# Orders in a three-layer fp32 kernel: the LayerNorm's variance, the RWKV pairs, the attention heads and the entry of S5

## The chip, the cores and the metric

The kernel runs on one NeuronCore of a Trainium2 chip, as one launch. The metric is the device time of one execution in microseconds (us), the median over runs. The engines are TensorE (PE in the profile, with its weight loads as PEld), VectorE (DVE), ScalarE (ACT), GpSimd (POOL) and SyncE (SP), which here only issues DMAs.

## The reference, cut to what matters

Input is x with 512 tokens of 1024 channels. All is fp32.

```python
x = first_block(x, ...)     # gMLP branch and RWKV-7 branch side by side
# second_block, two layers, each x = layernorm(alpha * x + gate * mixer(h)):
# i = 0: MLA attention over 512 latent and 256 context tokens, 16 heads; gives x and ctx
# i = 1: S5, 128 groups of 16 channels, 64 complex states, both directions; gives x only

def _layernorm(x, g, b):
    mu = mean(x); var = mean(square(x - mu))
    return (x - mu) * rsqrt(var + eps) * g + b

# RWKV-7, per head, per token:  S = S*w + (S a) b^T + v k^T ;  y = S r
# MLA, per head:  q_abs = q_nope @ w_uk ; p = softmax([q_abs, rope(q_r)] . keys) ; o = p . ckv
# S5, per group and direction:
#   u, g = split(h @ w_in); x_t = lam_bar * x_{t-1} + b_bar u_t ; y = Re(c x) + d u
#   out = (glu(gelu(y)) * silu(g)) @ w_out
```

## The kernel before, in words

Activations lie channel-major: 128 channels on the partitions, tokens along the free axis, eight blocks (k = 0 to 7) for 1024 channels. Weights come as a stream of 512 KB pieces through a ring of six slots, loaded by SP in one fixed order (L3175); a load waits until the slot's former piece has been used. Each engine's program is written out by hand in its own order, and `at(...)` gives the semaphore value at which a named step is done. No planner sets the order: moving a line moves the work.

**LayerNorm** (three of them, `LayerNorm`). Sums over channels are matmuls with a matrix of ones (`ones_product`, L335). `centre_dve` (L371) subtracts the mean per block, ScalarE squares it (L380), GpSimd adds squares in pairs (`pairs_pool`, L347) and TensorE sums the results into the variance (`var_pe`); ScalarE takes the root (L385), VectorE the reciprocal (L391) and scales each block (L395). The second one works on 768 columns (512 latent, 256 context tokens), the others on 512.

**RWKV.** Pairs of heads i = 0 to 3 in a software pipeline: `rwkv_pe`, `rwkv_act` and `rwkv_dve` work in iteration i on the chunk products of pair i, the eight-step state chain of pair i - 1 (`state_pe` L1220, `state_dve_` L1227), the preparation of pair i + 1, and batches of vector rows (`vec_rows_pe` L292: row vectors of the modulation, turned into columns by `vec_turn_pe` L303 and added by `vec_add_dve`). An iteration begins with four products (`products_pe`, L1026); VectorE masks them (`z0_dve`, RBT at L1163), and `akt_pe` (again L1026) waits for that. It ends with `gn_spread_pe` (L854), `gn_scale_dve` (L1300) and `gn_gain_act` (L1306), which finish the group norm of the pair before, and with the third vector batch. `rwkv_last_*` follow after iteration 3.

**Heads.** 16 heads, six units each: two units of 128 context queries and four of latent queries. Per unit TensorE makes scores (L2158, L2169), VectorE the maximum (L2275), ScalarE the exponential (L2295), VectorE the normalisation; TensorE turns the probabilities (`turn`, L2182) into PSUM banks 6 and 7, ScalarE copies them (`pt_act`: L2305 for the two context units, L2310), and TensorE multiplies by the values (L2193). The projection of the next head but one is woven in: fold (L2225), q_abs (L2229, copied by ScalarE at L2322, 768 columns) and rope (L2236). Both context units are turned into bank 6, so the second waits for the copy of the first. VectorE and GpSimd make S5's tables in the heads' free time; the products of b and powers of lambda are made per tile by `b_pow_dve` (L2019), stored to HBM by `b_pow_pool` (L2006) and loaded back for each tile of S5 by SP (L3081, 1 MB a tile).

**End of MLA.** The output projection (L2411), mean, then on VectorE: lags of tile 0 (`lags_dve`, L2650, L2653), one half of `b_pow_dve` for tile 15 (six 128x512 operations), centring, the other half, reciprocal. GpSimd's pair sums come before its last store; its memset (L2013) after all stores are done releases S5.

**S5.** 16 tiles m of 128 channels, each with four pairs n = 4m + pair. At the entry the scaled blocks are split into a rounded part and a rest (`s5_start_act`, L2497, L2501; `s5_start_dve`, L2523, L2515), and TensorE projects tiles 0 and 1 as they come (`u_project_pe`, L2575; 48 matmuls a tile, three products of hi and rest). Weights are rounded by ScalarE (L436) and their rests made by GpSimd (L448), two units a tile (`u_round_act`). ScalarE copies a projected tile to SBUF (`u_act`, L2590, L2592), SP stores it (L2604) and loads it transposed (L2613, eight DMAs). Per pair: `turn_pe` (L2669) transposes b powers, `x_pe` (L2715) makes the inputs of the states, `state_dve` (L2732 to L2752: multiply, scan, multiply) runs the recurrence, `y_pe` (L2769 with c powers; L2774 with u and the lag matrix) makes the output. The tile's lag matrix goes over HBM: TensorE (L2637), VectorE's copy (L2650), SP's store (L3154), and after it eight loads (L3161) that the tile's first L2774 waits for. In tile m TensorE also projects tile m + 2, split over the pairs by `TOKENS`; in tiles 14 and 15 these are the first two gate tiles (`gate_ahead_pe`). After the tiles come gates, GLU and output projection (L459), with ln3 at the end.

SP's program per tile: the 1 MB load of b powers for tile + 1, the lag store, the lag loads, u's store, c powers, table, u's loads, the ring's next piece.

## Time and profile before

| what | value |
|---|---|
| median of 3 runs | 2307.03 us (2306.19 to 2311.86) |
| profiled execution: own time, span | 2303.04 us, 2301.3 us |
| mean granted TensorE clock | 0.979 |
| busy: TensorE, VectorE, ScalarE, GpSimd | 93%, 58%, 34%, 27% of the span |
| first, second, third LayerNorm in the trace (us from the start) | 461 to 477, 1322 to 1355, 2276 to 2295 |
| RWKV iterations | 215 to 405 |
| heads | 692 to 1156, a head every 28.02 |
| S5 tiles | 1397 to 1742, a tile every 21.7 (first four), then 22.1 to 22.9 |
| after them: gates, GLU, output | 1749 to 2276 |

A row of a timeline reads: start, duration, engine, line, operation, what it writes <- what it reads, shape, how many; in brackets the idle time of the engine before it and what released it. A row of waits is: engine, waiting line <- releaser and its line, us in total, times, longest. PEclk is the share of the full TensorE clock (2.4 GHz) that was granted; 0.50 is the lower level. Durations of pipelined matmuls have modelled ends.

### The profile page before, as it was taken

What the parts mean: (1) busy time and instruction counts of PE and PEld (TensorE: products, weight loads), DVE (VectorE), ACT (ScalarE), POOL (GpSimd) and SP (SyncE); (2) the same over time, 40 slices, a digit from 0 to 9 for tenths busy, and PEclk for the clock granted to TensorE, in tenths of its full rate; (3) what the DMA queues carried; (4) which work ended last, traced back from release to release, by engine and by line L of the source; (5) the groups of instructions that cost most, each with busy time, mean ns of one, the idle gap of its engine ahead of it and who ended that gap; (6) DMA issues with size and microseconds to landing.
All of it is one profiled execution on the core that took longest, in us unless ns stands there. A gap on an engine that the chain in (4) does not pass through costs nothing.

```text
span 2301.3 us, 39928 instructions
## 1 busy us (share of the span) xinstructions
PE 2146.7 (93%) x15738; PEld 1559.2 (68%) x15738; DVE 1323.9 (58%) x2344; ACT 785.7 (34%) x1433; POOL 621.8 (27%) x1126
## 2 busy tenths in 40 slices
PE   6998998999998999999899958999998999999996
PEld 6876877755554555555455537888876788888784
DVE  2266664469994444444389877888884333333244
ACT  1335543231103444444300065454443423222223
POOL 0553211500017888888302111111110000000001
PEclk9999999999999999999999978999999999999998
DMA  8321443423451111111055316888874233333220
GB/s 309 101 90 57 150 150 119 159 82 115 170 188 56 67 53 51 51 54 67 35 207 182 144 61 188 257 248 264 247 235 176 83 93 100 94 98 100 93 92 37
DMA packets 105721, 294.58 MB, mean 128 GB/s; under 512 B 12608, under 2 KB 49728, under 8 KB 97088
## 3 DMA queue, kind: packets, MB, share of 16 engines
q1 hardware_dynamic: 93184, 227.02, 30.6%
q0 software_dynamic: 12352, 65.02, 7.5%
q8 instruction: 125, 2.05, 0.4%
q14 instruction: 60, 0.49, 0.1%
HBM read 225.01 MB, written 66.98 MB: 127 GB/s over the span
## 4 chain that ended last, share of the span: by engine, by line
PE 72%; DVE 13%; DMA 7%; issue 3%; ACT 3%; SPq 2%; POOL 0%; ACTq 0%; DVEq 0%; POOLq 0%
PE psum L459 29%; PE psum L2411 7%; PE psum L2193 4%; PE psum L2158 4%; DMA lags<-const 4%; DVE area L1933 3%; PE psum L2575 3%; PE psum L1040 3%; PE psum L2169 3%; PE psum L2236 2%; DVE dve_tmp L1933 2%; PE psum L2229 2%; PE psum L292 2%; SPq L3161 2%; PE psum L2182 2%
## 5 line engine op out<-in xcount | busy, mean ns | idle before, releaser
L459 PE MATMUL psum<-split,w_split 128*128 128x512 f32 x1632 | 373.2, 390 | 3.7 <-DVE w_split L441 3.7
L459 PEld LDWEIGHTS psum<-split,w_split 128*128 128x128 f32 x1632 | 307.4, 188 | 68.2 <-DVE w_split L441 4.1
L441 DVE TENSOR_TENSOR w_split<-ring,w_split 128x512 fp32r<-128x512 f32 x188 | 133.1, 708 | 319.0 <-ACT w_split L436 318.7
L1978 POOL TENSOR_TENSOR early<-early 128x8 f32<-128x8 f32 (+6 forms) x672 | 276.2, 411 | 52.8
L436 ACT ACTIVATE w_split<-ring 128x512 fp32r<-128x512 f32 x188 | 118.8, 632 | 349.4 <-PE psum L459 346.1
L1759 PE MATMUL psum<-early,ring 128*128 128x512 f32 (+1 forms) x544 | 176.5, 486 | 0.0
L2411 PE MATMUL psum<-gate,ring 128*128 128x512 f32 (+1 forms) x512 | 165.4, 486 | 1.2 <-issue 1.2
L2575 PE MATMUL psum<-h,u_w 128*128 128x256 f32 (+1 forms) x768 | 148.7, 347 | 14.1 <-ACT u_t L2497 13.6
L459 PE MATMUL psum<-h,w_split 128*128 128x512 f32 x624 | 148.2, 398 | 8.5 <-DVE w_split L441 8.5
L1759 PEld LDWEIGHTS psum<-early,ring 128*128 128x128 f32 x544 | 103.6, 191 | 71.8 <-issue 64.6
L2411 PEld LDWEIGHTS psum<-gate,ring 128*128 128x128 f32 x512 | 97.2, 190 | 69.3 <-issue 62.7
L459 PEld LDWEIGHTS psum<-h,w_split 128*128 128x128 f32 x624 | 118.4, 190 | 36.9 <-ACT w_split L436 5.4
L2575 PEld LDWEIGHTS psum<-h,u_w 128*128 128x128 f32 x768 | 119.7, 192 | 31.4 <-issue 14.9
L459 PE MATMUL psum<-h_split,in_w 128*128 128x512 f32 x600 | 139.1, 391 | 1.5 <-POOL in_w L448 1.5
L448 POOL TENSOR_TENSOR u_w<-ring,u_w 128x512 fp32r<-128x512 f32 x36 | 49.3, 1369 | 306.7 <-ACT u_w L436 306.4
L459 PEld LDWEIGHTS psum<-h_split,in_w 128*128 128x128 f32 x600 | 111.8, 188 | 27.2 <-ACT prev L704 2.1
L341 POOL TENSOR_TENSOR early<-xT 128x512 f32<-128x512 f32 x1 | 1.3, 1287 | 461.8 <-DVE xT L3052 461.8
L2275 DVE TENSOR_REDUCE early<-psum 128x1 f32<-128x768 f32 (+1 forms) x96 | 74.8, 780 | 75.6 <-PE psum L2169 73.6
L2158 PE MATMUL psum<-ckv,q_abs 128*128 128x256 f32 (+1 forms) x320 | 107.3, 475 | 5.9 <-ACT prob L2295 5.9
L448 POOL TENSOR_TENSOR in_w<-ring,in_w 128x512 fp32r<-128x512 f32 x50 | 77.2, 1543 | 125.8 <-ACT in_w L436 123.7
L2193 PE MATMUL psum<-area,ckv_tm 128*128 128x512 f32 (+1 forms) x256 | 102.8, 556 | 1.0 <-ACT area L2310 1.0
L2785 ACT ACTIVATE early<-psum 64x128 f32<-64x128 f32 x128 | 34.6, 270 | 159.7 <-PE psum L2774 100.5
(419 smaller groups left out, 3674.9 us busy)
## 6 DMA issues: line engine op xcount, KB each, us to landing
ring<-in_s_glu SPq DMA_DIRECT2D x64, 512.0 KB, 3.5
ring<-in_w_mod SPq DMA_DIRECT2D x48, 512.0 KB, 5.2
made_c_pow<-area POOLq DMA_DIRECT2D x16, 1152.0 KB, 5.2
c_pow<-made_c_pow SPq DMA_DIRECT2D x16, 1152.0 KB, 6.2
made_b_pow<-area POOLq DMA_DIRECT2D x16, 1024.0 KB, 4.6
b_pow<-made_b_pow SPq DMA_DIRECT2D x16, 1024.0 KB, 10.2
ring<-in_s_in SPq DMA_DIRECT2D x32, 512.0 KB, 6.1
ring<-in_w_in SPq DMA_DIRECT2D x29, 512.0 KB, 3.5
```

The lines of the kernel that those rows point to most:

```text
L436: nc.scalar.activation(rounded(buffer(u, 0)), source(u), ACT.Copy).then_inc(act_done, 1)
L441: nc.vector.tensor_tensor(rounded(buffer(u, 1)), source(u), buffer(u, 0), ALU.subtract).then_inc(dve_done, 1)
L448: nc.gpsimd.tensor_tensor(rounded(buffer(u, 1)), source(u), buffer(u, 0), ALU.subtract).then_inc(pool_done, 1)
L459: ins = nc.tensor.matmul(out, rounded(buffer(u, w)[:, ks]), values(x, k), start=(first and k == 0 and n == 0), stop=(last and k == UNIT_K ...
L1759: ins = nc.tensor.matmul(o, tile_w(("mla_in", m), k), h2[:, k, a:a + n], start=(k == 0), stop=(k == KD - 1))
L1933: nc.vector.tensor_tensor(o, a, b, op).then_inc(dve_done, 1)
L1978: nc.gpsimd.tensor_tensor(o, a, b, op).then_inc(pool_done, 1)
L2158: mm(o, q_abs_of(h, u), ckv[:, a:a + m], start=True, stop=False)
L2193: ins = mm(o, ckv_tm[:, k, :], pt[:, k, :], start=(k == 0), stop=(k == kt - 1))
L2275: v.tensor_reduce(sm[:, n % 3, 0:1], both(b)[:, 0:keys], AX.X, ALU.max).then_inc(dve_done, 1)
L2411: ins = nc.tensor.matmul(o, tile_w(("mla_out", 2 * m + k // KD), k % KD), gate2[:, k, a:a + n], start=(k == 0), stop=(k == KE - 1))
L2575: ins = nc.tensor.matmul(o, rounded(u_w[:, u % 4, w, kk * P:(kk + 1) * P]), h3_part(x, k)[:, a:a + size], start=(k == 0 and n == 0), stop= ...
```

## The change

Only orders, buffers and counts of small steps change; what is computed stays.

- **LayerNorm (all three).** GpSimd adds one pair of squares (4 and 5) instead of three pairs. TensorE sums seven blocks, in the order 0, 1, 2, 3, 6, the pair, 7, instead of five.
- **RWKV.** The turn of the third vector batch, its addition, and the spread, scale and gain of the group norm move from the end of an iteration behind the products (TensorE), behind z0 (VectorE) and behind the first `u_act_` (ScalarE) of the next one, or to the head of `rwkv_last_*`. State steps 1 to 3 are later in the order.
- **Heads.** The second context unit is turned into bank 7 and doesn't wait for the first one's copy. The copy of q_abs is two instructions (context 256 columns, latent 512); the first part of rope waits for the first only, the second part for both.
- **b powers of tile 15.** They are not made at MLA's end. `power_last_dve` keeps the powers in SBUF, SP loads b (b_last), and `b_pow_last_dve` makes the tile in SBUF in four groups of three 128x512 operations, behind the states of pairs 54 to 57 (tiles 13 and 14). The 1 MB store and load of that tile are gone. GpSimd adds ln2's squares after its last store has been issued.
- **S5 three tiles ahead.** TensorE projects tile 2 at the entry, before the first `x_pe`, and tile m + 3 in tile m; the gates come in tiles 13 and 14. ScalarE rounds unit 4 while the blocks are split, unit 5 between the copies of tiles 0 and 1, units 6 and 7 and the copy of tile 2 before `turn_act(1)`. GpSimd's rests and its y stores shift with that.

```diff
-    def pairs_pool(self, pool):
-        for j in range(KD // 2 - 1):
-            pool.wait_ge(*at(self.name, "sq", 2 * j + 1))
-            nc.gpsimd.tensor_tensor(self.sq[:, 2 * j, :], self.sq[:, 2 * j, :], self.sq[:, 2 * j + 1, :],
-                                    ALU.add).then_inc(pool_done, 1)
-            pool_count.up(self.name, "sq_pair", j)
+    def pair_pool(self, pool):
+        pool.wait_ge(*at(self.name, "sq", 5))
+        nc.gpsimd.tensor_tensor(self.sq[:, 4, :], self.sq[:, 4, :], self.sq[:, 5, :], ALU.add).then_inc(pool_done, 1)
+        pool_count.up(self.name, "sq_pair")
...
-        for j in range(KD // 2 - 1):
-            pe.wait_ge(*at(self.name, "sq_pair", j))
-            self.ones_product(self.var_bank, self.sq[:, 2 * j, :], j == 0, False)
-        for k in (KD - 2, KD - 1):
-            pe.wait_ge(*at(self.name, "sq", k))
-            ins = self.ones_product(self.var_bank, self.sq[:, k, :], False, k == KD - 1)
+        for k in (0, 1, 2, 3, 6, 4, 7):
+            if k == 4:
+                pe.wait_ge(*at(self.name, "sq_pair"))
+            else:
+                pe.wait_ge(*at(self.name, "sq", k))
+            ins = self.ones_product(self.var_bank, self.sq[:, k, :], k == 0, k == KD - 1)
...
     products_pe(pe, i)
+    if i > 0:
+        vec_turn_pe(pe, n0 - 1)
+    if prep:
+        prep_raw_pe(pe, i + 1)
+    if i > 1:
+        gn_spread_pe(pe, i - 2)
+    akt_pe(pe, i)
     if scan:
         state_pe(pe, i - 1, 1)
-    if prep:
-        prep_raw_pe(pe, i + 1)
-    akt_pe(pe, i)
+    vec_rows_pe(pe, n0, EARLY, *([("vec", n0 - 1, "added")] if n0 > FIRST_GATE else []))
+    u_pe(pe, i, 1)
     if scan:
         state_pe(pe, i - 1, 2)
-    vec_rows_pe(pe, n0, EARLY, *([("vec", n0 - 1, "added")] if n0 > FIRST_GATE else []))
-    u_pe(pe, i, 1)
     if prep:
         prep_k_ss_pe(pe, i + 1)
+    dz_pe(pe, i, 1)
     if scan:
         state_pe(pe, i - 1, 3)
-    dz_pe(pe, i, 1)
     vec_rows_pe(pe, n0, LATE)
...
         prep_turn_pe(pe, i + 1, 3)
-    if scan:
-        gn_spread_pe(pe, i - 1)
     if len(batches) == 3:
         vec_rows_pe(pe, batches[2], range(KD), ("vec", n1, "added"), *([("gn", i - 1, "std")] if scan else []))
-        vec_turn_pe(pe, batches[2])
...
-    if scan:
-        gn_gain_act(act, i - 1)
...
+    if i > 0:
+        vec_add_dve(dve, batches[0] - 1)
+    if i > 1:
+        gn_scale_dve(dve, i - 2)
+    zt0_dve(dve, i)
...
-    zt0_dve(dve, i)
+    if prep:
+        prep_scan_dve(dve, i + 1)
...
-    if prep:
-        prep_scan_dve(dve, i + 1)
...
+    vec_turn_pe(pe, TAIL_BATCH - 1)
+    gn_spread_pe(pe, q - 1)
...
-    for m in range(KE):
-        if m == KE - 1:
-            ln2.add_pool(pool, KD - 2)
-            ln2.pairs_pool(pool)
+    for m in range(KE - 1):
...
-        if m + 2 < KE:
+        if m + 2 < KE - 1:
...
-        if m % 2 == 1 and 5 <= m < KE - 1:
+        if m % 2 == 1 and 5 <= m:
...
+    ln2.add_pool(pool, KD - 2)
+    ln2.pair_pool(pool)
...
-        pool.wait_ge(b_pow_stored[i], 16 * KE // 2)
+        pool.wait_ge(b_pow_stored[i], 16 * (KE // 2 - i))
...
+power_last = const[:, len(MASKS) * P + N_LAGS + 8 * C_LAT + GS:][:, 0:2 * TPD * (STEP + 1)].rearrange(
+    "p (r t s) -> p r t s", r=2, t=TPD)
+b_last = const[:, len(MASKS) * P + N_LAGS + 8 * C_LAT + GS + 2 * TPD * (STEP + 1):][:, 0:N_B].rearrange(
+    "p (r t i) -> p r t i", r=2, i=GS)
...
+def power_last_dve(dve):
+    nc.vector.tensor_copy(power_last, power[:, :, tile_cols(KE - 1), :]).then_inc(dve_done, 1)
+    dve.wait_ge(dve_done, dve_count.up("s5", "power_last"))
...
+def b_pow_last_dve(dve, d, ri):
...
+    def tt(o, a, b, op):
+        nc.vector.tensor_tensor(o, a, b, op).then_inc(dve_done, 1)
+        dve.wait_ge(dve_done, dve_count.up("s5", "b_pow_last"))
...
+    if d == 0 and ri == 0:
+        dve.wait_ge(last_loaded, 16)
+        dve.wait_ge(*at("s5", "b_pow_t", TILE_PAIRS * (KE - 2) - 1))
+    shape = [P, TILE_PAIRS, STEP, GS]
+    part = s5_tmp[:, 0:TILE_PAIRS * STEP * GS].rearrange("p (t s i) -> p t s i", t=TILE_PAIRS, s=STEP)
+    idx = slice(7, None, -1) if d == 0 else slice(8, 0, -1)
+    pr, pi = (power_last[:, i, d::2, idx].unsqueeze(3).broadcast_to(shape) for i in range(2))
+    br, bi = (b_last[:, i, d::2, :].unsqueeze(2).broadcast_to(shape) for i in range(2))
+    out = b_pow[:, (KE - 1) % 2, ri, d::2, :, :]
+    if ri == 0:
+        tt(out, br, pr, ALU.mult)
+        tt(part, bi, pi, ALU.mult)
+        tt(out, out, part, ALU.subtract)
+    else:
+        tt(out, br, pi, ALU.mult)
+        tt(part, bi, pr, ALU.mult)
+        tt(out, out, part, ALU.add)
...
-        if n >= 1:
+        if n >= 1 and u != 1:
...
-            ins = nc.tensor.transpose(bank(6 + k // 3, (k % 3) * P, (k % 3 + 1) * P),
+            b = 6 + (u if u < 2 else k // 3)
+            ins = nc.tensor.transpose(bank(b, (k % 3) * P, (k % 3 + 1) * P),
...
-            pe.wait_ge(*at("q_abs", hh))
+            pe.wait_ge(*at("q_abs_ctx", hh))
...
+                if part == 1:
+                    pe.wait_ge(*at("q_abs", hh))
...
-                             bank(6, 0, 2 * P).rearrange("p (k c) -> p k c", k=2), ACT.Copy).then_inc(act_done, 1)
+                             bank(6 + u, 0, 2 * P).rearrange("p (k c) -> p k c", k=2), ACT.Copy).then_inc(act_done, 1)
...
-        nc.scalar.activation(q_abs[:, h % 2, :], both(0), ACT.Copy).then_inc(act_done, 1)
-        act.wait_ge(act_done, act_count.up("q_abs", h))
+        for (o, a, n), what in zip(parts_of(0), ("q_abs_ctx", "q_abs")):
+            nc.scalar.activation(q_abs[:, h % 2, a:a + n], o, ACT.Copy).then_inc(act_done, 1)
+            act.wait_ge(act_done, act_count.up(what, h))
...
             act.wait_ge(*at("s5", "h3", k - 2))
+        if k == 6:
+            u_w_act(act, 4)
         act.wait_ge(*at("ln2", "scaled", k))
...
         return
-    pe.wait_ge(*ready(b_pow_ready, m))
+    if m < KE - 1:
+        pe.wait_ge(*ready(b_pow_ready, m))
+    else:
+        pe.wait_ge(*at("s5", "b_pow_last"))
     if n == 0:
...
     turn_pe(pe, 0)
+    for k in range(KD):
+        u_project_pe(pe, 2, k)
     x_pe(pe, 0)
...
             for k in TOKENS[pair]:
-                u_project_pe(pe, m + 2, k)
+                u_project_pe(pe, m + 3, k)
             y_pe(pe, n)
...
     u_act(act, 0)
+    u_round_act(act, 5)
     u_act(act, 1)
...
         ln2_out_act(act, k)
-    u_round_act(act, 4)
-    u_round_act(act, 5)
+    u_round_act(act, 6)
+    u_round_act(act, 7)
+    u_act(act, 2)
     turn_act(act, 1)
...
-                u_round_act(act, 2 * (m + 3) + pair)
+                u_round_act(act, 2 * (m + 4) + pair)
...
-                u_act(act, m + 2)
+                u_act(act, m + 3)
...
-        if u % 2 == 1 and u >= 9:
-            y_store_pool(pool, u // 2 - 4)
-    for m in range(KE + GATES_AHEAD - 4, KE):
+        if u % 2 == 1 and u >= 11:
+            y_store_pool(pool, u // 2 - 5)
+    for m in range(KE + GATES_AHEAD - 5, KE):
...
+FIRST_LAST = TILE_PAIRS * (KE - 2) - 2
...
+            n = m * TILE_PAIRS + pair - FIRST_LAST
+            if 0 <= n < 4:
+                b_pow_last_dve(dve, n // 2, n % 2)
...
+            sp.dma_start(b_last, io["b_bar"][KE - 1].rearrange("p (r t i) -> p r t i", r=2, i=GS)).then_inc(last_loaded, 16)
...
-                b_pow_sync(sp, tile + 1)
+                if tile + 1 < KE - 1:
+                    b_pow_sync(sp, tile + 1)
...
+    power_last_dve(dve)
...
-    b_pow_dve(dve, KE - 1, (0,))
...
-    b_pow_dve(dve, KE - 1, (1,))
...
```

## Rows read from the trace of the kernel before

**Rows 1.** Span of the core and its granted TensorE clock.

```profile
...
core 0: 2301.3 us, clock 0.979
...
```

**Rows 2.** Page, parts 1 and 4: busy time by engine, then chain shares.

```profile
...
PE 2146.7 (93%) x15738; PEld 1559.2 (68%) x15738; DVE 1323.9 (58%) x2344; ACT 785.7 (34%) x1433; POOL 621.8 (27%) x1126
...
PE 72%; DVE 13%; DMA 7%; issue 3%; ACT 3%; SPq 2%; POOL 0%; ACTq 0%; DVEq 0%; POOLq 0%
...
```

**Rows 3.** PE's waits, whole run: line, releaser, us in total, times, longest.

```profile
...
PE psum L2575 <- ACT u_t L2497: 13.6, 1, 13.6
...
PE psum L2182 <- ACT area L2305: 10.3, 16, 2.4
PE psum L2774 <- DMA early<-lags: 9.9, 11, 2.3
PE psum L1026 <- DVE RBT L1163: 8.7, 4, 3.0
PE psum L335 <- POOL gate L347: 8.4, 1, 8.4
PE psum L2715 <- DMA u_t<-u_channels: 7.0, 1, 7.0
PE psum L2158 <- ACT prob L2295: 5.9, 16, 2.2
PE psum L2236 <- ACT q_abs L2322: 5.5, 16, 1.0
PE psum L335 <- POOL early L347: 4.0, 2, 3.7
...
```

**Rows 4.** Windows, S5 tiles 0, 7, 14: us, busy by engine, PEclk, DMA share, GB/s.

```profile
...
1396.92:1418.64 21.72, 21.72 (x250) 18.18 (x248) 17.58 (x41) 12.43 (x28) 2.62 (x2) 1.00 0.58 188
1550.64:1572.92 22.28, 21.79 (x248) 18.18 (x248) 18.86 (x47) 11.10 (x27) 3.30 (x3) 1.00 0.82 255
...
1708.27:1729.75 21.48, 19.15 (x224) 15.13 (x224) 18.37 (x51) 9.64 (x24) 2.45 (x3) 1.00 0.77 219
...
```

**Rows 5.** Timeline, start of an RWKV iteration: start, us, engine, line, idle before.

```profile
...
315.19 0.99 PE L1026 MATMUL psum<-a_cm,k_cm 64*64 64x64 f32 x32 [1.99 <-DVE RBT L1163]
...
```

**Rows 6.** Window over the RWKV iteration that begins there.

```profile
...
307.00:354.00 47.00, 42.81 (x1225) 37.33 (x1220) 30.08 (x56) 22.15 (x41) 9.01 (x10) 0.96 0.39 138
...
```

**Rows 7.** Timeline, first LayerNorm's variance.

```profile
...
467.79 4.46 PE L335 MATMUL psum<-sq,const 128*128 128x512 f32 x10
...
```

**Rows 8.** Timeline, third LayerNorm's variance.

```profile
...
2281.81 5.22 PE L335 MATMUL psum<-early,const 128*128 128x512 f32 x8 [0.26 <-POOL early L347]
...
```

**Rows 9.** Timeline inside one head.

```profile
...
903.87 0.44 PE L2182 MATMUL psum<-const,area 128*128 128x128 f32 x2 [0.52 <-ACT area L2305]
...
913.15 0.81 ACT L2322 ACTIVATE q_abs<-psum 128x768 f32<-128x768 f32 x1 [0.75 <-PE psum L2229]
...
```

**Rows 10.** Timeline, second LayerNorm up to the reciprocal.

```profile
...
1324.08 0.69 DVE L2019 TENSOR_TENSOR area<-area,power 128x512 f32<-128x512 f32 x1
...
1328.43 7.90 DVE L371 SCALAR_TENSOR_TENSOR early<-psum,early 128x768 f32<-128x768 f32 x8
...
1333.33 9.71 PE L335 MATMUL psum<-gate,const 128*128 128x256 f32 x20 [8.38 <-POOL gate L347]
...
1346.32 4.95 DVE L391 RECIPROCAL early<-early 128x768 f32<-128x768 f32 x1 [4.97 <-POOL area L2013]
...
```

**Rows 11.** Timeline in tile 7: a projection group, one operation's form alone and beside GpSimd.

```profile
...
1552.29 3.42 PE L2575 MATMUL psum<-h,u_w 128*128 128x256 f32 x18
...
1560.61 0.35 DVE L2724 TENSOR_TENSOR early<-early 128x192 f32<-128x192 f32 x1
...
1569.75 1.45 DVE L2724 TENSOR_TENSOR early<-early 128x192 f32<-128x192 f32 x1
...
```

**Rows 12.** SP's queue in the last tiles: lag store and lag loads.

```profile
...
1715.74 0.34 SPq L3154 DMA_DIRECT2D lags<-const  x1
1722.30 5.26 SPq L3161 DMA_DIRECT2D early<-lags  x8
...
```

More of the change, by code:

```diff
@@ L1431, in rwkv_act @@
             u_act_(act, i, 1)
+            if i > 1:
+                gn_gain_act(act, i - 2)
             if prep:
@@ L1564, in rwkv_last_act @@
             q = NPAIR - 1
+            gn_gain_act(act, q - 1)
             for k in range(3, 6):
@@ L1582, in rwkv_last_dve @@
             q = NPAIR - 1
+            vec_add_dve(dve, TAIL_BATCH - 1)
+            gn_scale_dve(dve, q - 1)
             for c in range(1, NCHUNK - 1):
@@ L2561, in u_project_pe @@
         def u_project_pe(pe, m, k):
+            if m >= KE + GATES_AHEAD:
+                return
             if m >= KE:
@@ L3061, in ln3_pool @@
                 ln3.add_pool(pool, k)
-            ln3.pairs_pool(pool)
+            ln3.pair_pool(pool)
         def ln3_pe(pe):
```

8 lines of the change are left out of this document (3 added, 5 removed).

## The prediction

> **What bounds the kernel now.** I read the span and granted clock first, then the page's busy shares and chain of waits, then TensorE's waits over the whole run, and only then timelines and windows around each edit. TensorE is busy 93% of the span, the clock is near full (0.979), and 72% of the chain that ended last is TensorE's [rows 1, 2]. So an edit is worth what it takes out of TensorE's idle time or puts into its work. The waits list shows how little idle there is and where it lies: one 13.6 us wait at the start of S5, one of 8.4 us in the second LayerNorm, one of 7.0 us for the transposed u, and many small ones in the heads, RWKV and the S5 tiles [rows 3]. The change touches nearly all of them. S5's tiles are not all alike: tile 0 has TensorE busy for its whole 21.72 us, tile 7 for 21.79 of 22.28 with the DMA engines 0.82 busy; there the late part is the load of the lag matrices, 9.9 us in 11 waits [rows 3, 4].
>
> **RWKV.** An iteration ends with the spread and scale of the pair before and with the turn of a vector row (`vec_turn_pe`), which waits shortly for ScalarE; in the next one `akt_pe` waits for VectorE's RBT: 1.99 us in the one shown, 8.7 us in four, the longest 3.0 [rows 3, 5]. The change puts the turn, the raw preparation and the spread behind the products, so their TensorE work fills the RBT wait. The spread is sixteen matmuls of the size of the 32 that took 0.99 us [rows 5], but narrow weights and twice the columns, so 1 us; the turn and its wait I take at 0.4 each: about 1.8 us an iteration where the wait is long enough. VectorE now runs z0 first and `gn_scale` (128x512, 0.69 us by the operation of that size in [rows 10]) after it, so RBT isn't later; but the scale delays the masks behind it (zt0) and the states. I take 0.75 for the iteration shown, 1.75 for each of the two after it, and some 1.6 for the clock: it stood at 0.96 over the 47 us shown [rows 6], which is 1.9 us a time, and it fell in just these idle gaps; I count one such loss and most of it again in the next; the last iteration loses 0.8, because the turn and spread now stand in front of its chain of state steps. Sum -5.0. Bounds: -6.5 (all four waits of 8.7 gone, less 2.2 for delayed masks) and -1.0 (the states, moved back on both engines, become what is late, so only the 0.40 waits go).
>
> **First LayerNorm.** Variance needs seven products instead of five. Ten matmuls took 4.46 us [rows 7], so one product (two matmuls) is 0.85 to 0.89. TensorE was the late engine there and stays it afterwards: +1.7; bounds 0 (if the last square was what held it) and +1.8. **Third LayerNorm.** Here the pair sum on GpSimd was late: two waits, 4.0 us together [rows 3], and the last eight matmuls took 5.22 us [rows 8], more than 8 x 0.446 = 3.6, a slow clock. Without the first two pair sums TensorE starts on single squares some 2 us sooner and ends, after 7 x 0.87 = 6.1 us, about 1.8 sooner. Bounds -2.3 and +0.8 (the same 7 products at the slower rate).
>
> **Heads.** Sixteen waits of `L2182` for the copy of the transposed probabilities (10.3 us, longest 2.4) come from two turns sharing one bank; the second turn gets its own bank and needn't wait. It is 0.52 us in the head shown [rows 9], of which I count 0.49: 15 x 0.49 + 0.65 for head 0, whose first turn is late for other reasons = 8.0. `L2236` waits for the whole copy of q_abs (5.5 us in 16) [rows 3]: the copy of 768 columns takes 0.81 us [rows 9]; its first third with a start cost will be ready some 0.4 sooner and the rope product needs only that: 15 x 0.28 + 0.43 = 4.6. Against it, ScalarE runs one more copy, about 0.17 to 0.2 us a head; it stands before the next exponential. TensorE reaches what follows later than ScalarE by about 0.5 us, which hides it. What is late next is `L2158` after the exponential, 5.9 us in 16, which I leave as it is. Sum -12.6; bounds -14 and -8 (every head gives back the extra copy and some 0.1 more at the exponential).
>
> **MLA's end.** The last b powers aren't made there: six VectorE operations of 0.69 us before the centring, and six after it, go, with their store [rows 10]. Added is one small copy at the start of the output projection, beside TensorE's own long work. Centring, which started at 1328.43, starts 3.4 us sooner, about 1325.05. The squares follow it at about 0.96 us each; seven products over 768 columns cost 7 x 0.89 x 1.5 = 9.3 us and start with the first square at about 1327: variance ends near 1336.6. Before, it began at 1333.33 behind the pair sums and ended at 1343.04, its twenty matmuls in 9.71 us where 5 x 1.33 = 6.7 would do, and the reciprocal then still waited for the store's memset until 1346.32 [rows 10]. Root and reciprocal now follow at about 1337.9: -8.4. If the clock falls in the sum, as it did before, half of that is lost, -4.3.
>
> **S5's entry.** The first projection starts 8.4 us sooner. TensorE then waited 7.0 us for u [rows 3]; now the whole projection of tile 2 stands in that wait. It is 48 matmuls, eighteen of which took 3.42 us with the modelled end of the last [rows 11], so 8.5 us: 1.5 beyond the wait. ScalarE gets a rounding step in its h chain (0.62 to 0.65, in one of the eight steps), and rounds and copies between the u copies. Against that, the x products and the first state group run without the slow clock that follows the idle 7 us, -2.1. The first y product, 1396.92 before (tile 0's window starts with it [rows 4]), comes at about 1387.9: -9.0 with the previous part. Bounds -10.5 and -4. Is it given back? The project work moved ahead leaves no shorter tile: in every tile TensorE does the same 48 matmuls for one tile further on, up to tile 12, and then the gates come one tile sooner. What remains unused is at tile 15, where VectorE holds the end anyway, so the gain stays until there.
>
> A collision counts here as well: the fifth rest on GpSimd (`L448`) now runs beside VectorE's h chain. In tile 7 a 128x192 operation of VectorE took 1.45 us with GpSimd's rest beside it, and 0.35 without [rows 11]. I leave it out of the sum and in the bounds: 1.1 once, with the start shared, 0.9.
>
> The Trainium skill, SBUF — State Buffer, "Who interferes with whom", says that a VectorE instruction with two SBUF inputs and a GpSimd instruction that reads SBUF exclude each other, and the later one waits for the whole of the first. The trace agrees with the 1.45 against 0.35. By this rule the moved rests would hit any such operation of VectorE, in the entry and in the tiles, which speaks against the change; by the rows the number of rests stays two a tile.
>
> **S5's end.** Twelve operations of 128x512, 0.69 us each [rows 10] plus gaps, 0.725: 2.18 a group, four groups in pairs 2 and 3 of tile 13 and 0 and 1 of tile 14. VectorE is busy 18.37 us in tile 14 and needs 4.4 more: 22.7 against its 21.48, with the state recurrence waiting behind each group [rows 4]. So this tile becomes VectorE-bound, +1.2 there, and +0.3 in tile 13. What is queued behind is the state group, TensorE's y product for it, and the copy of the last lags. The store of the last lags at 1715.74 is followed by loads only at 1722.30, 6.6 us later [rows 12], as the store's packets stood behind a 1 MB load of b powers, which is gone: that gives 2 to 5 us back to the last lag wait. I take -0.2 in all; bounds -2 and +5 (8.7 us less the 3 us that VectorE is idle in each tile, and no relief in the queue).
>
> **Sum.** -5.0 +1.7 -12.6 -9.0 -0.2 -1.8 = -26.9. The profiled execution took 2303.04 us, 1.74 around its span of 2301.3; it comes to 2276.1. The median of the runs shown is 2307.03, 4.0 above it, so 2280 is my number for the median.
>
> **Rivals.**
> (1) The lag chain keeps S5: in tiles 4 to 14 the DMA queue, not TensorE, sets the period [rows 4], and what the entry gains is partly taken by lags that land no sooner, and the b powers on VectorE cost the end 3.7 to 5. Then -26.9 + 4 to 5: -22, 2285. For it: the 9.9 us and DMA 0.82. Against it: the chain hangs on tile events that all move by the same 9 us.
> (2) The clock drops in the LayerNorm or the entry: -4.3 instead of -9.0, and in RWKV no relief (+1.6): -26.9 + 4.7 + 1.6 = -20.6, 2286. For it, the 9.71 us row [rows 10]; against it, TensorE is idle there for about 2 us only, not 8.
> (3) Heads keep their period, since the exponential's wait (`L2158`) takes up what the others give: -4 instead of -12.6: 2289. For it: ScalarE has one more instruction in front of the exponential. Against it: that wait is 5.9 us in 16 with one of 2.2 [rows 3], so about 0.25 in the others.
> (4) Slower than before: VectorE's chain becomes the bound of every S5 tile. It is busy 18.86 of 22.28 us [rows 4]; GpSimd's two rests a tile now start elsewhere, and each collision costs 1.1 [rows 11]. To cancel 27 us each of 16 tiles has to grow by 1.7, to 24.0, so that VectorE must lose 5.1 a tile, five collisions. With six a tile, 25.5 against 22.3 over the tiles, the time is 2303 - 27 + 51 = 2327 on the profiled execution; just past the point, 2310. For it: VectorE's slack is the smallest of the engines but TensorE's. Against it: there are two rests a tile, and one of them collides already.
>
> **How the numbers follow.** My forecast 0.55; rival 1 0.14, rival 2 0.12, rival 3 0.12, rival 4 0.04; and 0.03 for small gains that end up at no change. The range of the likeliest alone is 2274 to 2286. The range for the time is 2272 to 2291: it holds rivals 1 to 3 as well as several terms at their better end. A measurement of this kernel tells 0.3%, 7 us, from no change: faster 0.93, within 0.03, slower 0.04.
>
> **What would show it.** After: `L2182` no longer waits for `L2305` within a head, and the period of a head falls by about 0.77 (from 28.02); the `L1026` waits for RBT fall from 8.7 to under 4; the reciprocal `L391` of the second LayerNorm starts near 1338 less what RWKV and heads gave; no 7 us wait of `L2715`; first y product 25 us sooner than 1396.92; VectorE over 21 us busy in tile 14, and the lag store followed by its loads in under 4 us. Wrong if the head's period stays above 27.7, if the variance sum shows a clock of 0.5, or if tiles 1 to 12 are longer than 22.5 us.

## The result and the profile after

The changed kernel took 2283.27 us (median of 4 runs, 2279.60 to 2284.78), the kernel before 2308.28 in the runs beside it; the ratio is 0.9887, 95% interval 0.9863 to 0.9910, so 21 to 32 us less. Timed once more, it was 0.9891 (0.9873 to 0.9909). The forecast was 2280 in a range of 2272 to 2291. The profiled execution took 2281.87 us with a span of 2279.9. The total is right, in part by luck: several of its terms are off in opposite directions and cancel.

The first view is TensorE's waits over the whole run of the changed kernel: line <- what it waited for, us in total, times, longest. Line numbers have moved: L2620 was L2575, L2817 was L2769, L2195 was L2158, L1025 was L1026, L1219 was L1220.

```profile
PE psum L2620 <- ACT u_t L2540: 11.4, 1, 11.4
PE psum L2817 <- DVE const L2800: 9.4, 6, 2.2
PE psum L2195 <- ACT prob L2335: 5.8, 16, 2.2
...
PE psum L1025 <- DVE RBT L1162: 5.2, 3, 2.1
PE psum L1219 <- DVE states L1226: 4.4, 8, 0.9
...
PE psum L1025 <- issue: 2.9, 3, 1.4
...
PE psum L336 <- ACT early L379: 2.2, 2, 1.6
...
PE psum L336 <- ACT gate L379: 2.1, 1, 2.1
...
PE psum L2195 <- ACT dve_tmp L2335: 1.9, 1, 1.9
...
PE psum L2276 <- ACT q_abs L2363: 0.5, 1, 0.5
```

Against [rows 3]: the heads' wait for the copy of the probabilities (10.3) is gone, of the one for q_abs (5.5) 0.5 is left, and `L2195`, the exponential's, stands where it was, 5.8 for 5.9, plus one wait of 1.9 in the first head, where a wait of 2.4 for the copy stood. The 7.0 for u is gone, and so are all 9.9 us of waits for the lag matrices. Grown are the waits of the y product for VectorE's states (`L2800`), 9.4 us in six with the longest 2.2, where there was one of 1.1, and RWKV's for its states, 4.4 us for 2.0. The variance products (`L336`) now wait for ScalarE's squares, 4.3 us in three, where GpSimd's sums cost 12.4.

Windows over tiles 0, 7, 13, 14 of S5 after the change (us, busy by engine with counts, PEclk, DMA share, GB/s; they answer [rows 4]):

```profile
1379.61:1401.33 21.72, 21.72 (x250) 18.19 (x248) 19.47 (x48) 12.42 (x28) 2.54 (x2) 1.00 0.64 212
1531.70:1553.40 21.70, 21.70 (x250) 18.18 (x248) 18.79 (x47) 11.04 (x27) 3.35 (x3) 1.00 0.81 255
...
1661.00:1683.80 22.80, 20.64 (x227) 16.64 (x225) 21.84 (x51) 9.53 (x24) 2.80 (x3) 0.93 0.79 239
1683.80:1705.80 22.00, 18.60 (x217) 14.98 (x215) 21.04 (x55) 9.01 (x23) 0.54 (x1) 0.92 0.65 199
```

Tile 7 is TensorE's to the last tenth, as tile 0: no longer 22.28 with 21.79 busy. In tiles 13 and 14 VectorE is busy 21.84 of 22.80 and 21.04 of 22.00.

To see where the time went, I cut every profiled execution at the same instructions, each start read from its timeline. The first y product is the first `L2774` (`L2822` after the change), the last turn the first `L2793` (`L2841`) behind tile 15. Segment by segment in us, change and forecast with their signs:

| segment | before | after | change | forecast |
|---|---|---|---|---|
| start to RWKV's first products | 220.38 | 218.80 | -1.6 | 0 |
| to its last read-out | 184.90 | 188.93 | +4.0 | -5.0 |
| to the first LayerNorm's mean | 54.54 | 54.17 | -0.4 | 0 |
| its variance | 12.42 | 14.14 | +1.7 | +1.7 |
| to the first turn of the heads | 233.91 | 232.90 | -1.0 | 0 |
| heads | 445.97 | 431.92 | -14.1 | -12.6 |
| output projection of MLA | 169.04 | 169.04 | 0.0 | 0 |
| second LayerNorm to the first projection | 35.53 | 28.27 | -7.3 | -8.4 |
| to the first y product | 40.22 | 41.45 | +1.2 | -0.6 |
| S5 tiles 0 to 3 | 87.06 | 86.91 | -0.1 | 0 |
| tiles 4 to 11 | 179.11 | 173.81 | -5.3 | 0 |
| tiles 12 to 15, to the last turn | 79.69 | 79.50 | -0.2 | -0.2 |
| gates, GLU, projection | 531.71 | 534.80 | +3.1 | 0 |
| third LayerNorm's variance | 12.53 | 10.97 | -1.6 | -1.8 |

### The profile page after: what moved, and what is told of

It reads as the page before. It is cut to its first block, busy times and chain, and to the rows that moved or that the text cites. A ratio compares the mean times of both kernels' runs of the same rounds, so it can differ in the third digit from the quotient of the medians.

```text
span 2279.9 us, 39953 instructions
## 1 busy us (share of the span) xinstructions
PE 2152.7 (94%) x15754; PEld 1563.8 (69%) x15754; DVE 1319.6 (58%) x2345; ACT 788.1 (35%) x1449; POOL 613.6 (27%) x1118
## 4 chain that ended last, share of the span: by engine, by line
PE 88%; DVE 6%; issue 2%; ACT 2%; DMA 1%; POOL 0%; SPq 0%; DVEq 0%; ACTq 0%; POOLq 0%
PE psum L458 30%; PE psum L1764 8%; PE psum L2452 7%; PE psum L2620 5%; PE psum L2195 5%; PE psum L2231 4%; PE psum L2817 3%; PE psum L2206 3%; PE psum L1039 3%; PE psum L2220 2%; PE psum L2276 2%; PE psum L2267 2%; PE psum L2763 2%; PE psum L293 1%; PE psum L2822 1%
## 5 line engine op out<-in xcount | busy, mean ns | idle before, releaser
L2620 PE MATMUL psum<-h,u_w 128*128 128x256 f32 (+1 forms) x768 | 148.5, 348 | 13.0 <-ACT u_t L2540 11.4
L2620 PEld LDWEIGHTS psum<-h,u_w 128*128 128x128 f32 x768 | 119.8, 192 | 30.6 <-issue 12.7
L458 PEld LDWEIGHTS psum<-h_split,in_w 128*128 128x128 f32 x600 | 111.8, 188 | 27.2 <-ACT prev L703 2.1
L2195 PE MATMUL psum<-ckv,q_abs 128*128 128x256 f32 (+1 forms) x320 | 109.8, 474 | 8.2 <-ACT prob L2335 5.8
```

Of the source, the lines that this page charges most:

```text
L458: ins = nc.tensor.matmul(out, rounded(buffer(u, w)[:, ks]), values(x, k), start=(first and k == 0 and n == 0), stop=(last and k == UNIT_K ...
L2195: mm(o, q_abs_of(h, u), ckv[:, a:a + m], start=True, stop=False)
L2620: ins = nc.tensor.matmul(o, rounded(u_w[:, u % 4, w, kk * P:(kk + 1) * P]), h3_part(x, k)[:, a:a + size], start=(k == 0 and n == 0), stop= ...
```

## The experiments

**The change again**, unchanged.

> The changed kernel as it is, timed again on the chip of the three experiments beside it, so that each of them is read against it. All theories: ratio to the kernel before 0.987 to 0.991 (2280 to 2288 us).

0.9891 (0.9873 to 0.9909); median 2285.15, with 2276.23 to 2288.58 over five runs. Its profile has a span of 2274.3, 5.6 less than the first one. RWKV took 185.94 and the gates' stage 2.6 less; all other segments repeat within 0.1. Over all profiles of kernels that share a stage with this one the picture is less clean. The heads, the output projection, the variances of the first and third LayerNorm and, with three tiles ahead, tiles 0 to 11 repeat to 0.6 us or better. But the start takes 218.1 to 220.7, the stretch up to the heads 231.7 to 233.4, the second LayerNorm 27.4 or 28.3, and tiles 12 to 15 78.3 to 79.5, because the last one takes 13.0 to 14.1. RWKV can't be told to 3 us from one pair.

**RWKV's orders back** in the changed kernel, and **alone** in the kernel before.

```diff
 # rwkv_old (shown): the RWKV hunks of the diff reversed, in the changed kernel
 # rwkv_only: the same hunks, not reversed, in the kernel before
-            if i > 0:
-                vec_turn_pe(pe, n0 - 1)
+            if scan:
+                state_pe(pe, i - 1, 1)
             if prep:
                 prep_raw_pe(pe, i + 1)
-            if i > 1:
-                gn_spread_pe(pe, i - 2)
             akt_pe(pe, i)
...
```

> The changed kernel with the orders of RWKV as they were before, everything else changed. Theory A (the new order costs: the wait for RBT falls by 3.5 us, but states, the scale and more stalls at issue take 5): RWKV from its first products to its last read-out shrinks from 188.9 to about 185, and the whole is 3 to 5 us faster than the changed kernel. Rival B (the order gains what I forecast, and the loss in the one profile is clock drops and issue stalls that fall differently each time): 3 to 5 us slower than the changed kernel, the RBT waits back at 8.7.

> The kernel before with the orders of RWKV alone changed. Forecast on record: -5.0 us. Theory A (the waits for RBT fall by 3 us and the vector rows' by 1.2, but states, scale and stalls at issue take as much): within 0.1% of the kernel before. Rival B (the forecast; the profiles hide it under clock drops): ratio 0.998. Rival C (it costs, as the profile pair says, 4 us): ratio 1.001 to 1.002.

With the old orders the changed kernel has 0.9868 (0.9851 to 0.9884), not told apart from 0.9891; its segment took 189.4 us, not the 185 of theory A. The new orders alone have 1.0002 (0.9987 to 1.0017; 12 runs): no effect, and a gain of 5 us (0.9978) lies outside the interval; a loss of 4.0 (1.0017) stands just at its edge. All profiles say the same of the segment, first products to last read-out. New orders, nine profiles: 185.6, 185.9, 186.8, 188.3, 188.3, 188.9, 189.0, 193.4, 195.3; old orders, five: 184.9, 186.2, 189.4, 190.4, 192.0. The medians are 188.3 and 189.4. The spread is the clock's, above all: windows over the segment in the kernel before, then in the changed kernel's repeat, then in a kernel with the same orders from further down (SP late once, the first of them).

```profile
220.38:405.28 184.90, 161.66 (x4709) 140.52 (x4709) 105.53 (x205) 80.03 (x145) 34.49 (x40) 0.97 0.38 136
```

```profile
218.83:404.77 185.94, 161.63 (x4709) 140.24 (x4709) 105.21 (x205) 80.37 (x145) 35.41 (x40) 0.98 0.39 139
```

```profile
220.65:415.91 195.26, 170.58 (x4709) 148.34 (x4709) 105.97 (x205) 80.31 (x145) 33.23 (x40) 0.93 0.36 132
```

The same 4709 matmuls are busy 161.6 us at a granted clock of 0.98 and 170.6 at 0.93. What the order itself does is in the waits. Waits of this stretch in the changed kernel with the old orders, then in the changed kernel:

```profile
PE psum L1025 <- DVE RBT L1162: 8.7, 4, 3.0
PE psum L1039 <- issue: 4.2, 4, 2.2
PE psum L1219 <- DVE states L1226: 2.0, 5, 0.4
...
PE psum L304 <- ACT vec_row L1336: 1.6, 4, 0.4
...
PE psum L1025 <- issue: 1.5, 2, 1.3
```

```profile
PE psum L1025 <- DVE RBT L1162: 5.2, 3, 2.1
PE psum L1219 <- DVE states L1226: 4.4, 8, 0.9
PE psum L1025 <- issue: 2.9, 3, 1.4
...
PE psum L1039 <- issue: 1.3, 2, 1.0
...
PE psum L1219 <- DVE rkvg L1299: 1.0, 1, 1.0
...
PE psum L304 <- ACT vec_row L1336: 0.4, 1, 0.4
```

RBT gives back 3.5 and the vector rows 1.2, 4.7 together. The states take 2.4 and the scale (`L1299`) 1.0. The stalls at issue move: 1.4 more in the products (`L1025`), 2.9 less at `L1039`. They differ from execution to execution, so I took the mean over the profiles, new orders (nine) against old (five): RBT 5.8 for 8.5 and the vector rows 0.4 for 1.6, so 3.9 gained; the states 3.1 for 2.2, the scale 1.2 for none, all stalls at issue 10.9 for 10.0, so 3.0 lost. TensorE's whole idle time in the segment is 23.8 us for 24.5, and single profiles of either order lie between 22.3 and 26.1. What the new order leaves of its gain, 0.7 us, is smaller than that spread.

**The heads alone** in the kernel before.

```diff
-                if n >= 1:
+                if n >= 1 and u != 1:
...
-                pe.wait_ge(*at("q_abs", hh))
+                pe.wait_ge(*at("q_abs_ctx", hh))
```

> The kernel before with the edits of the heads alone (second context turn into bank 7, q_abs copied in two). My step: the heads' segment 12.6 us shorter; the changed kernel's profile shows 14.0. Theory A: 14.0 us here too, ratio to before 0.994, and the lag waits of S5 stay as before (9 to 11 us in some eleven waits). Rival B (part of the heads' gain came with the rest of the change): under 10 us.

0.9949 (0.9929 to 0.9969), 12 us; the heads' segment is 432.45 for 445.97, -13.5. Theory A, but for the lags: their waits are 16.2 us in nine in this profile, not 9 to 11, and its S5 tiles took 356.5 us for 345.9, so that its own time is only 4.4 us under the profiled one of before. With two tiles ahead the lag waits differ from execution to execution: 9.9, 16.2, 7.9 and 6.2 us in the four profiles.

**b powers of tile 15 made at MLA's end**, in the changed kernel.

```diff
-            power_last_dve(dve)
             mla_out_dve(dve)
             lags_dve(dve, 0)
+            b_pow_dve(dve, KE - 1, (0,))
             ln2.centre_dve(dve)
+            b_pow_dve(dve, KE - 1, (1,))
...
-                        b_pow_last_dve(dve, n // 2, n % 2)
```

> The changed kernel with the b powers of tile 15 made at the end of MLA as before (two halves around the centring, stored and loaded, no groups in tiles 13 and 14). By my sum: centring 4.3 us later (six operations), the reciprocal released by the store's memset, so the first projection 7 to 8 us later; in tiles 13 and 14 VectorE is freed of 8.7 us. Theory A (the end of S5 hardly pays for the groups): 6 to 8 us slower than the changed kernel. Rival B (the groups cost most of their 8.7 us at the end): within 2 us of the changed kernel.

The second LayerNorm to the first projection: 35.58 us, for 28.27 with the groups: +7.3, as in the kernel before. Tiles 12 to the last turn: 76.14 for 79.50, -3.4. So the groups in tiles 13 and 14 cost about half of what their removal from MLA's end brings, and by the segments they gain 3.9 us. The whole is 0.9896 (0.9878 to 0.9915), which isn't told apart from the changed kernel, as B had it; the segments, 3.9 us slower, lie between the two theories.

**Without the groups.** It leaves out the b powers of tile 15, and there is one execution of it.

```diff
-                if 0 <= n < 4:
-                    b_pow_last_dve(dve, n // 2, n % 2)
```

> The changed kernel without the four groups on VectorE; it leaves out the b powers of tile 15, so that tile computes with those of tile 13. Theory A (VectorE is what sets tiles 13 to 15): from tile 12 to the last turn 3.5 to 4.5 us shorter than the 79.5 of the changed kernel, below the 76.1 of the kernel with the powers made at MLA's end, whose 1 MB load makes the lags late. Rival B (the groups are hidden): within 0.5 us.

Tile 12 to the last turn 75.68, -3.8: theory A. It lies in one tile: tile 13 lasts 19.03 instead of 22.73 (22.6 to 22.7 in five profiles), tile 14 22.14 and 22.06. The last tile takes 13.82 here and 13.0 to 14.1 in the changed kernel and its repeats, so of the 8.7 us of VectorE's new work 2.6 to 3.8 are on the path. TensorE in tile 13, with the groups and then without them, at the product that waits for the states behind the first group, and the windows over the tile:

```profile
1675.49 1.93 PE L2817 MATMUL psum<-c_pow,const 64*64 64x128 f32 x16 [2.16 <-DVE const L2800]
```

```profile
1661.02:1683.75 22.73, 20.57 (x226) 16.58 (x224) 21.77 (x51) 9.53 (x24) 2.80 (x3) 0.92 0.79 239
```

```profile
1673.10 1.09 PE L2815 MATMUL psum<-c_pow,const 64*64 64x128 f32 x16
```

```profile
1660.79:1679.82 19.03, 19.03 (x226) 15.12 (x225) 18.27 (x47) 9.54 (x24) 2.81 (x3) 1.00 0.79 225
```

The wait is 2.16 us. The other 1.5 is the clock: from this product to the end of the tile the same matmuls take 8.26 us for 6.72, the product itself 1.93 for 1.09, at a granted clock of 0.92 over the tile for 1.00.

The missing 1 MB load of b powers is worth little: without groups on VectorE the stretch takes 76.14 with the load (the experiment before this one) and 75.68 without it, and there the last tile still waits once for its lags, 4.3 us.

**Two tiles ahead** instead of three, with the rounding steps, copies and y stores in their old places too, all else as changed.

```diff
-            for k in range(KD):
-                u_project_pe(pe, 2, k)
...
-                        u_project_pe(pe, m + 3, k)
+                        u_project_pe(pe, m + 2, k)
...
-                        u_act(act, m + 3)
+                        u_act(act, m + 2)
```

> The changed kernel with S5 two tiles ahead, as before: no projection of tile 2 at the entry, gates in tiles 14 and 15, rounding and copies in their old places; the b powers of tile 15 still in four groups on VectorE. Theory A (the third tile fills the wait for u and keeps the lag loads ahead): the 7 us wait of x_pe is back, lag waits of tiles 4 to 13 back, S5 from its first projection to its last turn 5 to 9 us longer than the 381.7 of the changed kernel. Rival B (the lag waits depend on how late SP is in tile 0, and that on chance): first y product 1.2 us sooner after the first projection (40.2 against 41.5), periods 21.72 for most tiles, and the last tile's end 1.5 to 3 us later, because the gates stand there: 0.5 to 2 us longer than the changed kernel.

0.9924 (0.9902 to 0.9945) for 0.9891. From the first projection to the last turn 389.4 us for 381.7: in this pair the third tile is worth 7.8 us. The first y product comes 0.8 sooner after the first projection, near what B had, but the waits for the lags are back, nine of them, 6.2 us, and tiles 4 to 11 take 179.8 for 173.8: A. The last tiles lose 2.6 more: 82.1 for 79.5, tile 14 alone 25.65 for 22.06. SP's queue in tile 5 of this kernel, and in tile 6 of the changed one (start, us of issue); the store of the lags (`lags<-const`) and the first of the loads behind it are what I call store to load:

```profile
1495.07 0.43 SPq L3228 DMA_DIRECT2D ring<-in_s_in  x1
1495.54 0.43 SPq L3132 DMA_DIRECT2D b_pow<-made_b_pow  x1
1498.25 0.32 SPq L3207 DMA_DIRECT2D lags<-const  x1
1506.74 3.63 SPq L3214 DMA_DIRECT2D early<-lags  x8
```

```profile
1512.37 0.43 SPq L3234 DMA_DIRECT2D ring<-in_s_in  x1
1513.71 0.34 SPq L3138 DMA_DIRECT2D b_pow<-made_b_pow  x1
1518.48 0.32 SPq L3213 DMA_DIRECT2D lags<-const  x1
1522.86 3.64 SPq L3220 DMA_DIRECT2D early<-lags  x8
```

In the first, the b powers go out 2.7 us before the lag store, and the store takes 8.5 us until the loads may start; in the second 4.8 us before it, and 4.4. Over tiles 5 to 12 store to load is 7.1 to 8.5 us in this kernel and 3.6 to 5.3 in the changed one. In all four profiles with two tiles ahead the waits are there, in all ten with three there are none before tile 13.

**Is it the wait for u?** SP held back in each tile until the time it had with two tiles.

```diff
             sp.wait_ge(*at("s5", "u", m))
+            if 2 <= m < KE - 1:
+                sp.wait_ge(*at("s5", "u", m + 1))
```

> The changed kernel with one wait added on SP: the store of u of tile m (2 to 14) also waits until ScalarE has copied tile m + 1, which is about the time at which it could be stored with two tiles of lead. Theory A (the lag waits of tiles 4 to 14 went because SP no longer waits for u in tile 0, so that its later transfers are early and don't stand in front of the next lag store): lag waits come back, periods of tiles 5 to 12 are 22.2 to 22.8 again, 5 us slower than the changed kernel. Rival B (the lag waits went for another reason, such as the different times of weights and rests): periods stay 21.72, no more than 1 us slower.

Tiles 4 to 11 in 173.81, 0.9880 (0.9863 to 0.9898): B. The store of u in tile 0 went at 15.75 us, as with two tiles (15.67), and store to load grew slowly, from 4.2 us for tile 4 to 5.9 for tile 12 and 7.0 for tile 13, where there is one wait, 0.5.

**SP late once.** Two kernels of this sort (a wait for pair 5's copy, then for pair 4's inputs) delayed nothing: the store of u went at 14.8 and 15.0 us.

> The changed kernel with one wait more on SP, once: the store of u of tile 2 waits for ScalarE's copy for pair 5, so that SP is some 3 us late in tile 0 and nowhere else. Theory A (DMA queue and SP are a loop that runs away once the ring's piece and the 1 MB of b powers are issued later than 3.74 us into a tile): store to load of the lags grows to 7 or 8 us by tile 4 and stays, lag waits of 0.4 to 1.1 us a tile, S5 4 to 6 us longer. Rival B (a late start is worked off): store to load back under 5 us within three tiles, no waits, no loss.

> The changed kernel with one wait more on SP, once: the store of u of tile 2 waits until VectorE has read the inputs of pair 4, 18.8 us into tile 0 instead of 14.8, so that SP is 4 us late once. (The earlier kernel of this sort waited for something that was there already, so it delayed nothing.) Theory A (DMA queue and SP are a loop that runs away once the ring's piece and the b powers are issued later than 3.74 us into a tile): store to load of the lags grows to 7 or 8 us and stays, with lag waits in tiles 4 to 13; from tile 4 to 12 the time is 177 to 180 instead of 173.8. Rival B (a late start is worked off, the third tile of lead itself keeps it stable): back under 5 us within some tiles, 173.8.

Both have 173.81 in tiles 4 to 11, which tells nothing of the question. The first, timed, has 0.9914 (0.9896 to 0.9933), which overlaps the changed kernel's interval, with RWKV at 195.3 us in its profile: so far can the same work spread. There is one execution of the second. The third kernel waits for the inputs of pair 5 and has RWKV and the first LayerNorm as before.

```diff
+            if m == 2:
+                sp.wait_ge(*at("s5", "x_read", 5))
```

> The changed kernel with RWKV's orders as before, the first LayerNorm with three pair sums and five products as before, and one wait more on SP, once: the store of u of tile 2 waits until VectorE has read the inputs of pair 5, 18.8 us into tile 0 by the last profile, where the store otherwise goes at 14.9: SP is 4 us late once. (Both earlier kernels of this sort waited for pair 5's copy and pair 4's inputs, which were there at 14.8 and 15.0: they delayed nothing, and their profiles are repeats of the changed kernel.) Theory A (SP and the DMA queue are a loop with two states, and the third tile only starts it on the good side): store to load of the lags grows to 7 or 8 us, waits in tiles 4 to 13, tile 4 to 12 in 177 to 180 us instead of 173.8. Rival B (the third tile itself keeps it stable): 173.8. First LayerNorm 12.4 us, not 14.1, under both. Whole: under B 0.985 to 0.987 of the kernel before, under A 0.987 to 0.990.

Now the store of u goes at 18.9 us. SP's queue after it, in tile 1:

```profile
1404.55 1.18 SPq L3247 DMA_DIRECT2D ring<-in_s_in  x1
1405.77 0.43 SPq L3151 DMA_DIRECT2D b_pow<-made_b_pow  x1
1409.07 0.32 SPq L3226 DMA_DIRECT2D lags<-const  x1
1415.51 3.64 SPq L3233 DMA_DIRECT2D early<-lags  x8
```

Store to load jumps from 1.7 to 6.4 us and stays at 6.1 to 7.2 through tile 12: the lateness of one tile is not worked off. But the loads of tiles 2 to 12 land 0.3 to 1.4 us ahead of their use (2.1 to 3.8 in the changed kernel), tiles 4 to 11 take 173.81, and only tile 13 waits, 0.7. So A is right that the loop of SP and its DMA queue keeps what it was given, and B that three tiles don't run into the wait. The first LayerNorm is 12.42, as expected. The whole is 0.9884 (0.9856 to 0.9913).

**A version without the groups and with both old orders**: b powers of tile 15 in the last turn of the output projection.

```diff
             for m in range(KD):
                 b_pow_dve(dve, 2 * m)
-                if m < KD - 1:
-                    b_pow_dve(dve, 2 * m + 1)
+                b_pow_dve(dve, 2 * m + 1)
                 dve.wait_ge(*at("mla_out", m))
```

> The changed kernel with three things otherwise: RWKV's orders as before; the first LayerNorm with three pair sums and five products as before; the b powers of tile 15 made and stored on VectorE in the last turn of MLA's output projection, as those of the other odd tiles are, so that neither MLA's end nor S5's tiles hold them. Theory A (VectorE has room in that turn: 17.4 us of powers in 20.6): first LayerNorm 1.7 us shorter, S5 from tile 12 to the last turn 3.5 us shorter than the changed kernel's 79.5, second LayerNorm as in the changed kernel; some 5 us faster than the changed kernel, ratio to before 0.985 to 0.988. Rival B (the last residual of the output projection comes late behind the powers, or the store delays the release of S5): the second LayerNorm takes back 2 us or more, and the ratio is that of the changed kernel, 0.989 to 0.991.

0.9889 (0.9868 to 0.9910): B. Tile 12 to the last turn is 74.75, -4.75, and the first LayerNorm 12.42, -1.7; but the second LayerNorm takes it back, 36.95 us to the first projection for 28.27. VectorE's last powers and the last residual (`L2477`), where the lag product that follows the output projection on TensorE began at 1313.28:

```profile
1317.77 0.69 DVE L2066 TENSOR_TENSOR area<-area,dve_tmp 128x512 f32<-128x512 f32 x1
1318.50 0.29 DVE L2477 TENSOR_SCALAR early<-ctxT 128x256 f32<-128x256 f32 x1
```

The residual stands some 5 us late behind the powers. My 17.4 of 20.6 had left out the residuals; the one of the turn before took 1296.79 to 1301.03, so a turn with both tiles' powers needs 21.6. No version here is told apart from the changed kernel as faster; the lowest ratio, 0.9868, is that with RWKV's old orders.

## Why the prediction was right in sum, and where it was wrong

The forecast for the profiled span was -26.9 us, the profile pair has -21.4, and the medians 25.0 apart lie between. RWKV missed 5 us or more and the second LayerNorm with the entry 2.9; the S5 tiles gave 5.4 more than forecast and the heads 1.5. That these errors cancel is luck.

**RWKV: forecast -5.0, measured none.** The step said that the turn and the spread fill the wait for RBT, with bounds -6.5 and -1.0. They do, 4.7 us of waits went in the pair shown and 3.9 in the mean. But the step counted one cost, 0.8 in the last iteration, and put the states that moved back on both engines and the stalls at issue at nothing; with the scale in front of the masks these cost 3.0 in the mean. "The states become what is late" stood as the bound, at -1.0; it was part of the case, and the result is zero. The 1.6 us for the clock was no term at all: the same program shows a segment of 185.6 to 195.3. Rival 2 had this part, no relief in RWKV.

**S5's tiles: forecast -0.2, measured -5.6.** The step held the lag chain's waits fixed, because all its events move by the same 9 us. The third tile takes them away: -5.3 in tiles 4 to 11, and two tiles ahead brings them back. In tiles 12 to 15 the -0.2 of the forecast is met by luck. The groups cost 2.6 to 3.8, where I had 1.5, and in tile 13, not in tile 14; against them the lag waits of these tiles went as well. The first half of rival 1 falls, since the lags gave nothing back, but its second half, a cost of 3.7 to 5 at the end, nearly came. Why tile 13 I read from VectorE's 21.84 of 22.80 us: the work fits only if no state ever waits. That is argued; shown are one wait of 2.16 us and 1.5 us of slow clock behind it. I had set the queue's relief at 2 to 5 us; the load that is gone is worth 0.5.

**Entry: forecast -0.6, measured +1.2.** The whole projection of tile 2 stands in the wait for u, as forecast. Piece by piece, before and after: the products of tiles 0 and 1 19.7 and 20.8 us; the wait for u's copies behind them 1.85 and 2.48, since a rounding step now stands between the copies; from the first turn to the first x product 7.58 and 10.47; from there to the first y product 11.12 and 7.75. The last two were my terms of 1.5 beyond the wait and 2.1 of relief; they measured 2.9 and 3.4. The windows over them, after, after and before:

```profile
1362.00:1372.00 10.00, 10.00 (x54) 8.58 (x54) 0.00 (x0) 5.69 (x9) 2.59 (x2) 0.85 0.33 88
```

```profile
1372.00:1379.60 7.60, 6.91 (x74) 5.65 (x72) 6.48 (x16) 3.48 (x7) 1.28 (x1) 1.00 0.50 155
```

```profile
1385.00:1397.00 12.00, 10.46 (x75) 8.68 (x76) 9.09 (x22) 2.51 (x5) 3.03 (x3) 0.62 0.40 118
```

The 48 matmuls of tile 2 take 9.92 us at this 0.85, where I had 8.5; they took 8.58 in one profile only, that of the last version above. What I left in the bounds is in the path, the first 1.1: the rest of unit 4 on GpSimd beside VectorE's split of the last blocks. Timeline of the changed kernel there:

```profile
1349.75 1.29 POOL L447 TENSOR_TENSOR u_w<-ring,u_w 128x512 fp32r<-128x512 f32 x1 [15.89 <-ACT u_w L435]
1349.84 2.01 DVE L2558 TENSOR_TENSOR h<-u_t,h 128x768 fp32r<-128x768 f32 x1
...
1351.91 2.36 PE L2620 MATMUL psum<-h,u_w 128*128 128x256 f32 x12 [1.18 <-DVE h L2558]
```

The same operation takes 0.96 alone and 2.01 here, and TensorE waits 1.18 for it. All ten profiles with three tiles ahead have 1.97 to 2.06 for it, all four with two tiles 0.96. The Trainium skill, SBUF — State Buffer, "Who interferes with whom", has this as an exclusive lock: the later of the two waits for the earlier. The trace agrees nearly: VectorE came 0.09 us after GpSimd's start and lost 1.05, where a full lock would take the remaining 1.20, my estimate from these rows.

**The second LayerNorm: forecast -8.4, measured -7.3.** Centring starts 3.9 us after the output projection instead of 7.3, -3.4 as worked out. The sum, and a window within it:

```profile
1315.74 10.99 PE L336 MATMUL psum<-gate,const 128*128 128x256 f32 x28 [2.06 <-ACT gate L379]
```

```profile
1318.00:1320.00 2.00, 2.00 (x4) 0.97 (x3) 1.93 (x3) 1.70 (x3) 0.00 (x0) 0.50 0.04 8
```

10.99 us where I had 9.3: the clock fell to the lower level in it for some 3.5 us, my estimate from the mean of 0.84 over the sum. It is 10.09 in six other profiles, at a granted clock of 1.00 in the one with RWKV's old orders, and there the segment is 27.4, so -8.2. Rival 2 in a small part.

**Right:** the heads, -14.1 (-13.5 alone) for -12.6: the wait for the first copy is gone in every head, the period fell from 28.02 to 27.2, and rival 3 falls, since the exponential's wait is what it was but for 1.9 in the first head. The first LayerNorm, +1.7, seven products in 6.17 us for five in 4.46, as forecast. The third, -1.6 for -1.8. Rival 4 falls: TensorE fills tiles 0 to 11.

**The signs.** Of those named beforehand, the heads' period and waits, the missing 7 us wait, VectorE's 21 us in tile 14 and the last lag store (loads 1.7 us after it) came. Three did not come out well: the RBT waits fell to 5.2, not under 4; the first y product came 17.3 us sooner, not 25; and the variance sum of the second LayerNorm did show a clock of 0.50, which was named as a sign of being wrong.

**Open.** Why the transfers of a tile take longer with two tiles ahead, at the same bytes and nearly the same times of issue (in tile 2 the b powers landed 9.6 us after their issue, against 8.0 in the kernel with SP held back, both issued 3.74 us into the tile), wasn't settled. The 3.1 us of the gates' stage are spread, not cause: from the gates' first product to the third mean 525.5 to 530.4 over all profiles, and the waits are the same before and after. The -1.6 at the start is spread as well: the kernel before with the heads' edit alone has 218.7 there.

## What to carry to other kernels

When a wait is filled by moving work, price what stood behind that work on each engine: here most of the 3.9 us gained in RWKV went to the states, the scale and stalls at issue. Price the clock with a new wait: 2.2 us of waiting in tile 13 cost 3.7. Before trusting one pair of profiles, cut it into segments at fixed instructions and look how each repeats: some repeat to 0.1 us, and one full of short dependent matmuls spreads by 10. Total the waits of a stretch before you balance a few of its rows. And a transfer loop that is late once can stay late; lead time put in front of it may be worth more than the time it fills.

## What the runs showed that I had not expected

The loop of SP and the DMA queue keeps a delay: 4 us late in one tile, 6.1 to 7.2 us from store to load in all that follow, for 2.7 to 5.3 without it, while the compute engines keep 21.72 us a tile through tile 11. Its loads still land before their use. And the granted clock differs between executions of one program at the same places: 0.93 to 0.98 over RWKV, worth 9 us.
